# Up-projection weights cast straight into freed slots, norm-2 loads on SyncE, and the last block in parts: a decoder layer on eight cores

## What is computed

```python
mod = silu(c) @ w_ada + b_ada                  # shift, scale, gate, twice
h   = rms_norm(x) * (1 + sc1) + sh1
q, f, i, g, B, C, h' = split(h @ w_in)         # 7 blocks of 512 columns
# HGRN2 heads (4 x 128x128 state), chunkwise; short convolution of width 3
mix = concat[rmsnorm(o_hgrn) * gain * silu(g), B * conv3(C * h')] @ w_out
x   = x + g1 * mix
h2  = rms_norm(x) * (1 + sc2) + sh2
x   = x + g2 * (relu(h2 @ w_up)**2 @ w_down)   # D_FF = 4096
y   = rms_norm(x) * g_final
```

## Time and profile before

| | us |
|---|---|
| median of 3 runs | 915.79 (915.34 to 917.19) |
| the profiled execution, all | 917.29 |
| its span on the slowest core, 0 | 915.4 |
| spans of the eight cores | 898.6 to 915.4 |
| TensorE busy in that span | 828.4 (90%) |
| VectorE, ScalarE, GpSimd busy | 477.7, 368.7, 181.4 |

### The profile page before, as it was taken

The page is one execution under the profiler, slowest core; times in us unless marked ns, Lnnn a source line. Parts: engine busy times, 40 slices in busy tenths (PEclk is TensorE's granted clock), DMA queues, the critical chain, the costliest instruction groups (busy, mean ns, idle before and its releaser), DMA issues.

```text
span 915.4 us, 16894 instructions; the slowest of 8 cores (898.6 to 915.4 us)
## 1 busy us (share of the span) xinstructions
PE 828.4 (90%) x5919; PEld 520.1 (57%) x5973; DVE 477.7 (52%) x888; ACT 368.7 (40%) x782; POOL 181.4 (20%) x236
## 2 busy tenths in 40 slices
PE   1579899999797999956999999999999999999995
PEld 1447686686574867633554565455446545654852
DVE  1376896486995768583451445244524533442421
ACT  2267862365773767441330333134223312311411
POOL 3110134432654114132101201100110021011001
PEclk9989999999998999978999999999999999999998
DMA  9999909799889997899995302210211012002001
GB/s 161 191 195 193 216 2 163 216 191 220 286 194 128 214 154 84 285 179 233 179 191 152 136 3 70 92 47 1 101 61 47 24 47 92 1 2 92 25 1 46
DMA packets 27870, 112.46 MB, mean 123 GB/s; under 512 B 3814, under 2 KB 4326, under 8 KB 22028
## 3 DMA queue, kind: packets, MB, share of 16 engines
q0 software_dynamic: 6336, 42.04, 29.8%
q1 hardware_dynamic: 17420, 54.67, 18.6%
q10 hardware_dynamic: 4032, 14.68, 5.3%
HBM read 127.86 MB, written 30.81 MB: 173 GB/s over the span
## 4 chain that ended last, share of the span: by engine, by line
PE 78%; DMA 8%; issue 5%; DVE 4%; ACT 3%; POOL 1%; POOLq 0%; ACTq 0%; DVEq 0%; SPq 0%
PE B L481 76%; DMA adaf<-w_ada 5%; DMA xn<-x 2%; DMA recs<-Sl 2%; ACT W L508 2%; PE B L492 2%; DVE W L525 1%; DVE hT L521 0%; DVE W L519 0%; POOL mix L515 0%; DVE W L529 0%; ACT A L508 0%; DVE Sd L515 0%; DVE W L515 0%; POOL xr L515 0%
## 5 line engine op out<-in xcount | busy, mean ns | idle before, releaser
L481 PE MATMUL B<-h2T,wup 128*128 128x384 bf16 (+1 forms) x1536 | 239.1, 319 | 7.6 <-DVE h2T L521 7.5
L481 PE MATMUL B<-wdn,uT 128*128 128x512 bf16 x1061 | 234.7, 379 | 1.4
L508 ACT ACTIVATE W<-B 128x384 f32<-128x384 f32 (+2 forms) x241 | 118.6, 495 | 244.8 <-PE B L481 235.6
L481 PE MATMUL B<-hT,win 128*128 128x256 bf16 (+1 forms) x1728 | 200.8, 274 | 5.7 <-DMA win<-w_in 4.8
L481 PEld LDWEIGHTS B<-h2T,wup 128*128 128x128 bf16 x1536 | 150.7, 98 | 96.0 <-issue 10.9
L515 POOL TENSOR_TENSOR xr<-xr,W 128x512 f32<-128x512 f32 x68 | 88.8, 1308 | 455.9 <-DVE W L515 440.1
L481 PEld LDWEIGHTS B<-hT,win 128*128 128x128 bf16 x1728 | 162.1, 100 | 29.7 <-issue 6.5
L481 PEld LDWEIGHTS B<-wdn,uT 128*128 128x128 bf16 x1088 | 105.9, 98 | 124.9
L515 DVE TENSOR_TENSOR uT<-W,B 128x384 bf16<-128x384 f32 (+1 forms) x192 | 100.7, 531 | 127.7 <-ACT W L508 121.7
L515 DVE TENSOR_TENSOR W<-B,Gp 128x512 f32<-128x512 f32 x64 | 43.7, 687 | 121.8 <-PE B L481 120.5
L481 PE MATMUL B<-wout,mix 128*128 128x512 bf16 x265 | 65.3, 403 | 19.8 <-POOL mix L515 19.1
(11 more groups left out here) (139 smaller groups left out, 631.4 us busy)
## 6 DMA issues: line engine op xcount, KB each, us to landing
x<-xr SPq DMA_DIRECT2D x17, 512.0 KB, 11.4
xn<-x ACTq DMA_DIRECT2D x17, 512.0 KB, 7.5
xr<-x SPq DMA_DIRECT2D x17, 512.0 KB, 3.6
ada<-w_ada POOLq DMA_DIRECT2D x8, 1024.0 KB, 13.6
xr<-xp SPq DMA_DIRECT2D x16, 512.0 KB, 7.6
wscr<-w_up POOLq DMA_DIRECT2D x8, 1024.0 KB, 20.5
wdn<-w_down POOLq DMA_DIRECT2D x8, 1024.0 KB, 26.1
wup<-wscr SPq DMA_DIRECT2D x8, 1024.0 KB, 18.8
```

The source lines that it names most:

```text
L481: ins = e.matmul(o_, lhsT=l_, rhs=r_, start=st, stop=sp_, skip_group_check=True)
L508: return P.op("act", lambda e: e.activation(out=out, in_=in_, func=func, **kw), r, w, c, prio=prio)
```

## The change

The diff, cut to what matters:

```diff
+    POOL_SLACK = 3000.0
...
-                if o.dma is not None:
+                if q.dma is not None and q.eng == "pool" and o.dma is None:
+                    x = now + self.LAT[o.eng] + self.POOL_SLACK
+                elif o.dma is not None:
...
+    m0 = a0 + 32768
...
+    h2T0, _ = place("h2T0", [128, 8, 384], BF16, offset=m0)
...
-    def convert(i, after):
-        dma("pool", wscr_d[i], wup_d[i], [], ["wscr%d" % i], 1.5 * MB2, after=after)
-
-    up_ops = {}
-
     def load_up(j):
-        up_ops[j] = dma("sp", flat(wup[j]), wscr_d[j], ["wscr%d" % j], [wup_n[j]], MB2 / 2)
+        dma("pool", flat(wup[j]), wup_d[j], [], [wup_n[j]], MB2)
 
     def load_dn(j):
-        gate = up_ops.get(4 if j == 2 else 7)
-        dma("pool", flat(wdn[j]), wdn_d[j], [], [wdn_n[j]], MB2, after=[gate] if gate else ())
+        dma("pool", flat(wdn[j]), wdn_d[j], [], [wdn_n[j]], MB2)
...
-                tt("pool", mx[:, h0:h0 + NH, t0:t0 + 128], R_[...
+                tt("dve" if last else "pool", mx[:, h0:h0 + NH, t0:t0 + 128], R_[...
...
-                tt("pool", xr[:, sl], xr[:, sl], W[:], ALU.add, [xrn, Wn], [xrn])
+                tt("dve" if last else "pool", xr[:, sl], xr[:, sl], W[:], ALU.add, [xrn, Wn], [xrn])
...
-    def norm2(blocks):
+    def norm2(blocks, h2T, pre):
         for s, blk in enumerate(blocks):
-            nbv, nbn = normed(x1_d[blk], ["x1_%d" % blk])
+            nbv, nbn = normed(None, None, fetch(x1_d[blk], ["x1_%d" % blk], None, "sp"))
...
+        def finish(s):
+
+            x, xn = xr[s]
+            sums = []
+            pieces = [(0, 512, "pool"), (512, 768, "dve"), (768, 1024, "dve")]
+            for c0, c1, eng in pieces:
+                bank, bn = GB.take()
+                dh, h0 = c0 // 512, c0 % 512
+                for a in range(4):
+                    mm([(bank[:, 0:c1 - c0], uT[:, upos[a * 8 + k], s * 128:(s + 1) * 128], wdn[dh * 4 + a][:, k, h0:h0 + c1 - c0],
+                         a == 0 and k == 0, a == 3 and k == 7) for k in range(8)],
+                       ["uT%d" % (a * 8 + k) for k in range(8)] + [wdn_n[dh * 4 + a]], [bn])
+                W, Wn = WB.take()
+                tt("dve", W[:, 0:c1 - c0], bank[:, 0:c1 - c0], Gp[:, c0:c1], ALU.mult, [bn, "Gp"], [Wn])
+                tt(eng, x[:, c0:c1], x[:, c0:c1], W[:, 0:c1 - c0], ALU.add, [xn, Wn], [xn])
+                s_, sn = stR.take()
+                act(W[:].bitcast(BF16)[:, 0:c1 - c0], x[:, c0:c1], AF.Square, [xn], [Wn, sn], accum=s_[:])
+                sums.append((s_, sn))
+                if c1 < 1024:
+                    tt("pool", x[:, c0:c1], x[:, c0:c1], gfin_b[:, c0:c1], ALU.mult, [xn, "gfin_b"], [xn])
+            (a_, an), (b_, bn), (s_, sn) = sums
+            tt("dve", a_[:], a_[:], b_[:], ALU.add, [an, bn], [an])
+            ts("dve", a_[:], a_[:], 1.0 / 1024, EPS, ALU.mult, ALU.add, [an], [an])
+            act(s_[:], s_[:], AF.Ln, [sn, an], [sn], scale=1.0 / 1024, bias=a_[:])
+            act(s_[:], s_[:], AF.Exp, [sn], [sn], scale=-0.5)
+            blk = blocks[s]
+            rows = yp_d[blk * 128:(blk + 1) * 128, :]
+            y, yn = xnR.take()
+            stt(y[:, 768:1024], x[:, 768:1024], s_[:], gfin_b[:, 768:1024], ALU.mult, ALU.mult, [xn, sn, "gfin_b"], [yn])
+            ts("dve", y[:, 512:768], x[:, 512:768], s_[:], None, ALU.mult, None, [xn, sn], [yn])
+            z, zn = xnR.take()
+            act(z[:, 0:512], x[:, 0:512], AF.Copy, [xn, sn], [zn], scale=s_[:])
+            dma("act", rows[:, 0:512], z[:, 0:512], [zn], ["y%da" % blk], 128 * 2048)
+            dma("sp", rows[:, 512:1024], y[:, 512:1024], [yn], ["y%db" % blk], 128 * 2048)
...
-            if step == "R":
-                ends = {o.wn: o for o in P.ops[t0op:] if o.eng == "pe" and o.wn[0] == "O"}
-                for b, o in enumerate(ends.values()):
-                    for _ in range(CONV.count((n_, b))):
-                        convert(UPORD[conv_i], [o])
-                        conv_i += 1
             if step == "B" and n_ + 1 == len(tiles):
...
-                norm2(bgroups[0])
+                norm2(bgroups[0], h2T0, "h2T0_")
...
-    for j in range(2, 8):
+    for j in (2, 3, 4, 6, 7):
         load_dn(j)
     WT = WB
     for n_, bl in enumerate(bgroups):
-        up(bl)
+        up(bl, *((h2T, "h2T") if n_ else (h2T0, "h2T0_")))
+        if n_ == 0:
+            load_dn(5)
         if n_ + 1 < len(bgroups):
-            norm2(bgroups[n_ + 1])
+            norm2(bgroups[n_ + 1], h2T, "h2T")
```

More of the change, by code:

```diff
@@ L465, in assemble @@
     convp_d = dout("convp", [128, 4, 2]); recs_d = dout("recs", [16, 128, 512]); convs_d = dout("convs", [128, 4, 32])
-    wscr_d = nc.dram_tensor("wscr", [8, 128, 4160], BF16, kind="Internal").ap()[:, :, 0:4096]
     x1_d = nc.dram_tensor("x1", [17, 128, 1024], F32, kind="Internal").ap()
@@ L666, in assemble @@
         P.buf("h2T%d" % s, (w0 + 6 * 2048, w0 + 9 * 2048), group="h2T")
+    h2T0, _ = place("h2T0", [128, 8, 384], BF16, offset=m0)
+    for s in range(3):
+        P.buf("h2T0_%d" % s, (m0, m0 + 6144), group="h2T0")
     xnR = Ring("xn", 2, [128, 1024])
@@ L1091, in mixer_tile @@
                 h0 = heads[0]
-                tt("pool", mx[:, h0:h0 + NH, t0:t0 + 128], R_[:, h0 * 128:(h0 + NH) * 128].rearrange("p (h t) -> p h t", t=128),
+                tt("dve" if last else "pool", mx[:, h0:h0 + NH, t0:t0 + 128], R_[:, h0 * 128:(h0 + NH) * 128].rearrange("p (h t) -> p h t", t=128),
                    sg[g][0][:].rearrange("p (h t) -> p h t", t=TT)[:, :, t0:t0 + 128], ALU.mult, [rn, sg[g][1]], [mxn[hd] for hd in heads])
@@ L1173, in mixer_tile @@
                 tt("dve", W[:], bank[:, :], G[:, sl], ALU.mult, [bn, gn], [Wn])
-                tt("pool", xr[:, sl], xr[:, sl], W[:], ALU.add, [xrn, Wn], [xrn])
+                tt("dve" if last else "pool", xr[:, sl], xr[:, sl], W[:], ALU.add, [xrn, Wn], [xrn])
             dma("sp", x1_d[xblk + b], xr[:], [xrn], ["x1_%d" % (xblk + b)], 128 * 4096)
-    def norm2(blocks):
+    def norm2(blocks, h2T, pre):
         for s, blk in enumerate(blocks):
-            nbv, nbn = normed(x1_d[blk], ["x1_%d" % blk])
+            nbv, nbn = normed(None, None, fetch(x1_d[blk], ["x1_%d" % blk], None, "sp"))
             if blk == SAMPLE:
-                sample_mod(nbv, nbn, h2T, "h2T%d" % s, s * 128, 16, 24)
+                sample_mod(nbv, nbn, h2T, pre + "%d" % s, s * 128, 16, 24)
                 continue
@@ L1188, in norm2, with up @@
                 ts("dve", h2T[:, j, s * 128:(s + 1) * 128], Mb[:, j * 128:(j + 1) * 128], modT[:, 24 + j, 0:1], modT[:, 16 + j, 0:1],
-                   ALU.mult, ALU.add, [Mn, "modT2", "modT3"], ["h2T%d" % s], mode=1.0)
-    def up(blocks):
+                   ALU.mult, ALU.add, [Mn, "modT2", "modT3"], [pre + "%d" % s], mode=1.0)
+    def up(blocks, h2T, pre):
         N = 128 * len(blocks)
@@ L1195, in up @@
             mm([(bank[:, 0:N], wup[fc // 4][:, k, (fc % 4) * 128:(fc % 4 + 1) * 128], h2T[:, k, 0:N], k == 0, k == 7) for k in range(8)],
-               [wup_n[fc // 4]] + ["h2T%d" % s for s in range(len(blocks))], [bn])
+               [wup_n[fc // 4]] + [pre + "%d" % s for s in range(len(blocks))], [bn])
             W, Wn = WB.take()
@@ L1243, in down @@
             for s in range(len(blocks)):
+                if blocks[s] == 15:
+                    finish(s)
+                    continue
                 for dh in range(2):
@@ L1254, in assemble @@
     hs = {}
-    CONV = [(4, 0), (5, 0), (5, 1), (6, 0), (6, 1), (7, 0), (7, 1), (8, 0)]
     bgroups = [[SAMPLE, 0, 1], [2, 3, 4], [5, 6, 7], [8, 9, 10], [11, 12, 13], [14, 15]]
-    conv_i = 0
     late = []
@@ L1318, in assemble @@
     for n_ in range(3, len(tiles)):
-        t0op = len(P.ops)
         if n_ + 1 < len(tiles):
```

## The result

| | before | after |
|---|---|---|
| median of the runs beside each other, us | 916.42 | 906.06 (905.9 to 906.3) |
| ratio, 95% interval | 1 | 0.9888 (0.9871 to 0.9906) |
| span of the slowest core, us | 915.4 (core 0) | 904.6 (core 3) |
| median of die 0, of die 1, us | 909.0, 906.3 | 900.5, 899.8 |

The gain is 10.4 us; the forecast was 20 (896.0).

What follows compares the result with a forecast made beforehand. TensorE is fully busy from 511.7 to 904.8 us, so gains lie ahead of it: 915.4 - 11.6 - 15.4 + 3 - 2.1 = 889.3, plus 5 for spread and 1.9 outside the span, 896 us; range 884 to 914.

Steps and rivals of the forecast that it cites:

- Holes of the mixer: TensorE's waits for mix near 285 and 353 us close without the converts: 3.7 + 7.9 = 11.6 us gained.
- the spread of the cores: Slowest core stood 6.4 us above its die's median; nothing makes the cores more alike, so 5 us added.
- The hole at 397 us: TensorE mostly idle from 397 to 425.3 us, slow clock after; 22.4 us at most, 7 left, 15.4 gained.
- up-projection matmuls can fill the wait for mix: Within the 397 us hole: h2T0's slots free early, so the first blocks need no longer wait for tile 8.
- SyncE's queue: Norm-2 loads move there from ScalarE's queue; what queues behind them was costed at 0.
- a late transfer in VectorE's queue: Rival, 0.18: waits for xr loads or norm-2 scalings stall VectorE 10 to 18 us in the first up-projection; 906 to 914.
- The stream: Twelve cast loads of w_up and w_down at 8.5 us each end at 470 us; 3 us lost.
- the work alone is the limit: Rival, 0.12: loads come at 6.9 us or VectorE keeps up, with less spread; 884 to 889 us.
- the third rival: Rival, 0.13: weight loads bound the first down-projection, from 10.8 us a load; at 11.5 us a load, time 925.
- The tail: Last block finished in parts after the last matmul: saves 2.3, smaller matmuls cost 0.2, net 2.1 us.
- those of being right: Include first h2T0 matmul by 405 us, wdn5 landed by 475, first down-projection ended at 485 to 495.
- the signs of being wrong: TensorE waiting over 5 us for wup or wdn, VectorE for xr, GpSimd on TensorE, or steady-part holes behind SyncE.

Runs made afterwards that it cites:

- run 4: Changed kernel with only w_up's way undone (eight casts into DRAM scratch during the mixer, bf16 loads by SyncE): 931 and 935 us, ratio 1.018.
- run 8: Changed kernel with the planner's 3 us of slack for GpSimd's DMA issues taken out: 899.3 us, ratio 0.9814.
- run 5: Changed kernel without h2T0: first group's norm 2 goes into the old h2T, wdn5 loaded in its place before wdn6: 906.9 us, ratio 0.9899.
- Run 9: Changed kernel with the convp store packed and the first group's norm 2 emitted earlier within the last tile: 897.1 us, ratio 0.9792.
- run 11: Kernel before the change with only the convp store packed, 128 packets of 32 bytes: 908.6 us, ratio 0.9916.
- Run 1: Changed kernel with the convp store packed, 128 packets of 32 bytes instead of 512 of 8: 899.7 us, ratio 0.9813.
- run 12: Kernel of run 9 with the two w_down loads ahead of the last cut to half, output not the reference's: 888.3 us, ratio 0.9689.
- run 7: Changed kernel with the last block finished like the others, in halves of 512 columns and one store: 908.9 us, ratio 0.9923.

## Why the prediction was half right

*Holes of the mixer: 11.6 taken, less 5 for the spread of the cores.* The last projection of the slowest core ends 5.8 us earlier, where these two terms together had 6.6. On a typical core (median of eight, 392.4 against 388.9) it is 3.5 us. The waits for mix of the earlier trace rows are gone, and runs 4 and 8 fit the mechanism. Of the 11.6 the 7.9 was core 0's own bad luck: the wait of 6.2 us stands on no other core, the one of 2.2 us on all eight. The spread was sized well: the slowest core is 4.1 us above its die's median, where 5 was added.

*The hole at 397 us: 15.4 taken.* This is the step that failed, in two places: 2.4 us came of it. First, "up-projection matmuls can fill the wait for mix" was true of the buffers and not of the order. The planner kept the output projection first, so TensorE still waits 5.6 us for mix and 2.8 for h2T, and starts at a lower clock (16 matmuls in 5.93 us, 3.62 warm); with h2T0 free and nobody using it, run 5 without it is as fast. Run 9, which gives that order, has neither wait. From the projections' end to the up-projection it still takes 19.1 us where the sum had 8.1 + 7 = 15.1: 4.0 us short. Second, the up-projection became 6.7 us longer (51.2 instead of 44.5 on these cores), 6.1 of wait and some slow clock, where I had put a gain of 2.2: 8.9 short. Together 13 of the 15.4.

*SyncE's queue: costed at 0.* I listed what stands behind the three loads on that queue and not what stands ahead of them. The store of convp is ahead, and it was in the diff's surroundings all the time, 27.6 us to landing in the kernel before (run 11). Run 1 puts its price at 6.3 us. Of the rivals "a late transfer in VectorE's queue (906 to 914)" names this kind of stall, the 906.1 lies at its lower end, and its clause on the norm-2 scalings is near; but the queue was ScalarE's, and the load x1 of the second group, not xr.

*Yet the store isn't a new cost.* Run 11 shows that it cost the kernel before as much, 7 us, by another way: transfers of all rings were slower, and with them the load behind the 14.4 us of the earlier trace rows. With the store packed on both sides the change is worth 0.9813 / 0.9916 = 0.9896, so 9.5 us, about the 10.4 that it has as it stands. My explanation after the first comparison, that a new stop had eaten the gain, was therefore half the story: core 0's 28.2 us from the projections' end to the up-projection held some 6 us that were the store's (22.4 in run 11), I counted them as gained, and they came back in the next stage. Between the slowest cores of runs 11 and 1 the same landmarks give 4.9 in the mixer, 3.3 in the hole, -1.4 and -1.3 in the two stages behind it (the -1.3 again the eight matmuls done early) and 4.1 from there to the end, 9.6 us.

*The stream: 3 taken.* In the kernel after it cost nothing. The second group starts at 505.3, 43.6 us behind the down-projection's start, where it was 42.1, but these 1.5 us are the eight matmuls of the second group done before it, and the next stage gives them back; TensorE waits for no load. The rows' 8.5 us a load (1.05 MB as bf16) held: from 400 to 453 us the cast ring moved 7.37 MB, 7.5 us a load, and in run 9 from 453 to 482 us 3.56 MB, 8.5 us. But that the stream cost nothing was due to the other stops: the last load landed at 479.9, and TensorE came to it at 489.8. Take them away, and it binds at once: 4.9 to 7.8 us in run 9, and run 12's 888.3, with the stream relieved, lies in the 884 to 889 of "the work alone is the limit". The 925 of the third rival didn't come, since no load took 10.8 us on the average.

*The tail: 2.1 taken,* 2.9 measured in the traces, 2.9 in run 7. From the last matmul to the end it is 7.7 us instead of 10.6. The 0.2 us taken off for the smaller matmuls don't follow from the rows: 64 of 256 columns take 7.15 us there and 32 of 512 columns 2 x 3.62 = 7.24.

*Its signs.* Of those of being right, three didn't come: the first matmul on h2T0 stands at 410.5 us and behind the output projection, the last w_down load landed at 479.9 instead of by 475, and the down-projection ended at 505.5. None of the signs of being wrong named the wait that did come, ScalarE's for x1 of the next group.

*The range* held the time because the rival of the late transfer was let into it; the forecast itself, 889 to 902, did not. That 906 is inside is partly luck: the rival's stall was right in kind, and wrong in its engine and its transfer.

## What to carry to other kernels

Before a load is moved to another queue, list what is *ahead* of it on that ring, in packets and not in bytes: a store of 4 KB in 512 pieces held a ring for 25 us beside cast loads, and storing it in 128 pieces gained 6 to 7 us in both kernels, in the kernel before on a load that wasn't on that ring. A free buffer doesn't fill a hole; the order does, and it must be looked for in the matmuls' order, not assumed of a planner. And when stops are removed one after the other, price the next bound with the others gone: here a down-projection that started 9 us earlier brought 2.7 us, because the stream of weights stood behind it.

The best version measured that computes all of it is that of run 9: 897.1 us, 0.9792 of the kernel before.

## What the runs showed of the hardware

Packets of different rings take turns one by one. From 400 to 453 us the kernel after moved 1011 packets on q0 and 1013 on q1, 7.37 against 1.69 MB; run 1 956 and 954. While convp's packets run (401.7 to 426.8 us, core 3) it is clearest:

```profile
q0 software_dynamic: 543, 3.92, 100.7%
q1 hardware_dynamic: 545, 0.05, 3.5%
```

Equal counts alone would also come of turns of several packets each. But of the 8 KB cast packets that begin from 402 to 426 us, 96% begin within 8 ns after an 8-byte packet has begun, where chance would give 15%. A ring's speed beside others is therefore set by its packet size: convp's 512 packets are 32 for each of 16 engines, and 24.9 us / 32 = 0.78 us for each, about the 0.80 us that one cast packet takes. The Trainium skill's "DMA: Bandwidth & Descriptors" (Queues, rings and completion order) has the DMA engines alternate between rings by packets of some 9 to 17 descriptors. That they alternate agrees; turns of that length don't, by the order of the packets here. For SyncE's queue it makes no difference: in either form convp's 32 pieces on an engine wait for about as many cast packets, an estimated 32 x 0.8 = 26 us. So it shouldn't have been costed at 0.

A store in 8-byte pieces slows other transfers too. In run 11, against the kernel before, 128 pieces of 32 bytes in place of 512 of 8 raised what the DMA engines moved in 400 to 418 us: between 273 and 313 GB/s on the eight cores instead of between 156 and 212, at the same share of about 1.0.

The cost of an idle stretch is more than its length. After the 5.6 us of wait for mix the next 16 matmuls took 5.93 us instead of 3.62; after the 5.5 us at 482 us in run 9 the next 72 took 17.18 instead of 15.70.
